# Down product of an expert block run one block later, behind gate and up of the next

## The reference, cut to what matters

```
def expert_block(args):
    xb_i, e = args
    h = jax.nn.silu(xb_i @ w_gate[e]) * (xb_i @ w_up[e])
    return h @ w_down[e]
yb = lax.map(expert_block, (xb, blk_e))
return jnp.zeros_like(x2d).at[t_s].add(yb[dest] * w_s[:, None])
```

## Time and profile before

| | us |
|---|---|
| median of 3 runs | 1984.62 (1983.09 to 1987.86) |
| time of the profiled execution | 1987.03 |
| its span, first to last instruction | 1985.3 |
| sixteen first blocks, sum of their lengths | 304.50 |
| sixteen second blocks | 297.59 |
| eight third blocks | 145.36 |

### The profile page before, as it was taken

One profiled execution on the slowest core, in us unless ns is written; L12 is line 12 of the kernel. 1 busy time (PEld: TensorE's weight loads), 2 busy tenths in 40 slices (PEclk: granted clock), 3 DMA queues, 4 the chain that ended last, 5 costly groups with the idle time before them and its releaser, 6 DMA issues. The chain is left out here.

```text
span 1985.3 us, 29116 instructions
## 1 busy us (share of the span) xinstructions
PE 1885.8 (95%) x10232; PEld 1609.0 (81%) x10233; DVE 1059.1 (53%) x2070; ACT 751.6 (38%) x1408; POOL 412.3 (21%) x571
## 2 busy tenths in 40 slices
PE   7899999999999999999999954999999999999996
PEld 5899987788888788888888853888888888888885
DVE  5634343545444654455453335576677666565572
ACT  4332323333334233333333213444465444444451
POOL 2000000000201001000001013444444434434443
PEclk9899999999999999999999956999999999999998
DMA  7222233422245223333223425587678857655552
GB/s 225 87 86 86 86 130 106 154 77 93 87 148 195 81 88 104 127 128 106 85 87 105 170 86 191 190 288 255 221 247 287 296 203 260 218 194 204 193 179 92
DMA packets 166566, 309.97 MB, mean 156 GB/s; under 512 B 18448, under 2 KB 85008, under 8 KB 166490
## 3 DMA queue, kind: packets, MB, share of 16 engines
q1 hardware_dynamic: 133706, 223.61, 32.8%
q0 software_dynamic: 32784, 85.33, 12.4%
HBM read 256.13 MB, written 83.69 MB: 171 GB/s over the span
## 5 line engine op out<-in xcount | busy, mean ns | idle before, releaser
L64 PE MATMUL bank<-xT_hi,wh 128*128 128x512 f32 (+1 forms) x960 | 340.8, 355 | 7.4 <-ACT S L751 5.4
L65 PE MATMUL bank<-xT_lo,wh 128*128 128x512 f32 (+1 forms) x960 | 340.4, 355 | 0.0
L66 PE MATMUL bank<-xT_hi,wl 128*128 128x512 f32 (+1 forms) x960 | 339.3, 353 | 0.0
L799 DVE TENSOR_TENSOR wl<-raw,wh 128x512 fp32r<-128x512 f32 x352 | 219.3, 684 | 201.7 <-ACT wh L602 201.6
L1776 PE MATMUL bank<-gu_hi,ex_hi 128*128 128x256 f32 (+1 forms) x960 | 313.9, 327 | 5.7 <-DVE gu_lo L1651 5.7
L1778 PE MATMUL bank<-gu_hi,ex_lo 128*128 128x256 f32 (+1 forms) x960 | 306.3, 319 | 0.0
L1777 PE MATMUL bank<-gu_lo,ex_hi 128*128 128x256 f32 (+1 forms) x960 | 306.2, 319 | 0.0
L602 ACT ACTIVATE wh<-raw 128x512 fp32r<-128x512 f32 x352 | 192.1, 619 | 85.2 <-PE bank L1223 54.7
L64 PEld LDWEIGHTS bank<-xT_hi,wh 128*128 128x128 f32 x960 | 182.3, 190 | 36.2 <-issue 9.8
L1776 PEld LDWEIGHTS bank<-gu_hi,ex_hi 128*128 128x128 f32 x960 | 182.7, 190 | 29.9 <-DVE gu_lo L1651 12.1
L66 PEld LDWEIGHTS bank<-xT_hi,wl 128*128 128x128 f32 x960 | 182.5, 190 | 25.5
(11 more groups left out here) (239 smaller groups left out, 3275.5 us busy)
## 6 DMA issues: line engine op xcount, KB each, us to landing
raw<-in_w_in SPq DMA_DIRECT2D x56, 1024.0 KB, 5.1
raw_gate_up<-in_w_gate SPq DMA_DIRECT2D x16, 2048.0 KB, 8.2
raw_gate_up<-in_w_up SPq DMA_DIRECT2D x16, 2048.0 KB, 9.5
raw_d<-in_w_down SPq DMA_DIRECT2D x16, 2048.0 KB, 10.1
raw<-in_w_out SPq DMA_DIRECT2D x16, 1024.0 KB, 6.3
raw<-in_w_up_pool SPq DMA_DIRECT2D x16, 512.0 KB, 3.4
raw<-in_w_up_gmlp SPq DMA_DIRECT2D x16, 512.0 KB, 4.6
h<-in_x_prompt SPq DMA_DIRECT2D x16, 512.0 KB, 5.0
```

What stands on the lines that cost most here:

```text
L64: nc.tensor.matmul(out, lh, rh, start=(i == 0), stop=False)
L65: nc.tensor.matmul(out, lh, rl, start=False, stop=False)
L66: last = nc.tensor.matmul(out, ll, rh, start=False, stop=(i == n - 1))
L799: lo = lambda out, x, hi: tt(out, x, hi.bitcast(F32), ALU.subtract)
```

## The change

The diff has these parts:

- PE: `down(j - 1)` stands behind gate, up and the row transposes of block j. All four hidden transposes of block j come after it, into one bank. Block 0 is written out ahead of the loop and has no down product; after the loop one more `down(total - 1)` follows.
- Up is one pass of 24 products of 512 columns into one bank, and hid is made by one DVE instruction once up is done.
- ACT and DVE make the parts of the transposed hidden rows of block j - 1 (`hidden_high`, `hidden_low`) in block j, in one instruction each. In a first block these stand behind the splits of gate and up.
- The down weights of a new expert are split at the end of its first block: ACT waits until the last down product of the expert before is done (`y_done`), since it now comes in that block.
- DVE: `scale(j + 1)` and then `rows_low(2 * j + 3)` stand behind hid in every block, first ones too, and the down split behind both.
- POOL: one more index tile and copy in each step (idx_2), and one more round at the end, since the rows lag by one block more.

```diff
@@ phase_three, POOL
+                    nc.gpsimd.tensor_copy(idx_2[:, :], idx_1[:, :]).then_inc(moved_2, 1)
+                    wait_apart(pool, moved_2, j, passed_pool)
                     nc.gpsimd.tensor_copy(idx_1[:, :], idx[:, :]).then_inc(moved, 1)
...
-                out_landed(total + 1)
-                wait_apart(pool, z_ok, 2 * total + 2, passed_pool)
...
+                for last, n in ((False, total + 1), (True, total + 2)):
+                    out_landed(n)
+                    wait_apart(pool, z_ok, 2 * n, passed_pool)
+                    nc.gpsimd.tensor_copy(idx_y[:, :], idx_h[:, :]).then_inc(moved_y, 1)
+                    root(n)
+                    wait_apart(pool, moved_y, n, passed_pool)
+                    if not last:
+                        next_h(n + 1, idx_1)
+                    store_final(n)
@@ phase_three, ACT
+                def hidden_high(j):
+                    act.wait_ge(th_done, j + 2)
+                    nc.scalar.activation(hT[0][:, :, :], bankH[:, :].rearrange("p (k i) -> p k i", k=KH),
+                                         ACT.Copy).then_inc(hT_hi, 1)
+
                 def per_block(e, i, lo, j, first=False):
+                    hidden_high(j - 1)
                     if not first:
                         use_sigmoid_table(0)
                         square(j + 1)
                     act.wait_ge(g_done, j + 1)
                     nc.scalar.activation(sg[:, :], bankG[:, :], ACT.Sigmoid).then_inc(sg_ok, 1)
+                    rows_high(j + 2)
                     if first:
+                        act.wait_ge(down_in, 16 * i + 16)
+                        act.wait_ge(y_done, lo + 2)
+                        for k in range(KH):
+                            nc.scalar.activation(dn[0][:, k, :], raw_d[:, k, :], ACT.Copy).then_inc(e_hi, 1)
@@ phase_three, DVE
                     if not first:
                         add(j + 1)
-                        mean(j + 1)
+                    hidden_low(j - 1)
+                    mean(j + 1)
                     dve.wait_ge(sg_ok, j + 1)
                     tt(sg[:, :], bankG[:, :], sg[:, :], ALU.mult)
                     dve.drain()
-                    dve.wait_ge(u1_done, j + 1)
...
+                    dve.wait_ge(gu_done, j + 2)
+                    tt(hid[:, :], bankU[:, :], sg[:, :], ALU.mult).then_inc(hid_ok, 1)
+                    scale(j + 1)
+                    rows_low(2 * j + 3)
                     if first:
...
+                        for k in range(KH):
+                            dve.wait_ge(e_hi, SPLITS_ACT * i + 2 * KD + k)
+                            lo_half(dn[1][:, k, :], raw_d[:, k, :], dn[0][:, k, :]).then_inc(e_lo, 1)
@@ phase_three, PE
+                def down(j):
+                    pe.wait_ge(z_ok, 2 * j + 4)
+                    pe.wait_ge(hT_lo, j + 2)
+                    for k in range(KH):
+                        for half in range(2):
+                            last = accumulate(bankY[half][:, :], hT, k, dn, k, slice(half * HALF, (half + 1) * HALF),
+                                              k, KH)
+                    last.then_inc(y_done, 1)
...
                     for k in range(KD):
                         pe.wait_ge(e_lo, SPLITS * i + KD + k + 1)
+                        last = accumulate(bankU[:, :], xT, k, gu, KD + k, slice(0, HALF), k, KD)
                     last.then_inc(gu_done, 1)
                     rows_of_x(16 * j + 32)
...
+                    if not begin:
+                        down(j - 1)
+                    hidden_transposed(j)
+                per_block(0, 0, 0, 0, first=True, begin=True)
+                experts(pe, lambda e, lo: None, per_block, peel=True, skip_first=True)
+                total = pe.value_load(blk_tab[0:1, 2 * NE - 1:2 * NE], min_val=1, max_val=MAXBLK)
+                down(total - 1)
```

More of the change, by code:

```diff
@@ L1627, in per_block @@
                     nc.scalar.activation(sg[:, :], bankG[:, :], ACT.Sigmoid).then_inc(sg_ok, 1)
[L1628 to L1639, removed]
+                    rows_high(j + 2)
                     if first:
-                        rows_high(j + 2)
+                        act.wait_ge(down_in, 16 * i + 16)
+                        act.wait_ge(y_done, lo + 2)
+                        for k in range(KH):
+                            nc.scalar.activation(dn[0][:, k, :], raw_d[:, k, :], ACT.Copy).then_inc(e_hi, 1)
                 experts(act, split, per_block, peel=True)
                 total = act.value_load(blk_tab[0:1, 2 * NE - 1:2 * NE], min_val=1, max_val=MAXBLK)
+                hidden_high(total - 1)
                 square(total + 1)
+                square(total + 2)
             @block.vector
@@ L1734, in per_block @@
                     dve.drain()
-                    dve.wait_ge(u1_done, j + 1)
[L1736 to L1739, removed]
-                    if first:
[L1741 to L1754, removed]
+                    dve.wait_ge(gu_done, j + 2)
+                    tt(hid[:, :], bankU[:, :], sg[:, :], ALU.mult).then_inc(hid_ok, 1)
+                    scale(j + 1)
+                    rows_low(2 * j + 3)
+                    if first:
+                        for k in range(KH):
+                            dve.wait_ge(e_hi, SPLITS_ACT * i + 2 * KD + k)
+                            lo_half(dn[1][:, k, :], raw_d[:, k, :], dn[0][:, k, :]).then_inc(e_lo, 1)
                 experts(dve, split, per_block, peel=True)
                 total = dve.value_load(blk_tab[0:1, 2 * NE - 1:2 * NE], min_val=1, max_val=MAXBLK)
-                add(total + 1)
-                mean(total + 1)
-                scale(total + 1)
+                hidden_low(total - 1)
+                for n in (total + 1, total + 2):
+                    add(n)
+                    mean(n)
+                    scale(n)
             @block.tensor
@@ L1778, in accumulate, with hidden_transposed, per_block @@
                     return nc.tensor.matmul(out, a[1][:, ka, :], w[0][:, kw, cols], start=False, stop=(n == total - 1))
[L1780 to L1783, removed]
+                def hidden_transposed(j):
+                    pe.wait_ge(hid_ok, j + 1)
+                    for k in range(KH):
+                        last = nc.tensor.transpose(bankH[:, k * P:(k + 1) * P], hid[:, k * P:(k + 1) * P], ident[:, :])
                     last.then_inc(th_done, 1)
[L1786 to L1791, removed]
+                def down(j):
+                    pe.wait_ge(z_ok, 2 * j + 4)
+                    pe.wait_ge(hT_lo, j + 2)
+                    for k in range(KH):
+                        for half in range(2):
+                            last = accumulate(bankY[half][:, :], hT, k, dn, k, slice(half * HALF, (half + 1) * HALF),
+                                              k, KH)
+                    last.then_inc(y_done, 1)
+                def per_block(e, i, lo, j, first=False, begin=False):
                     pe.wait_ge(ex_lo, 2 * j + 2)
-                    pe.wait_ge(hT_lo, 2 * j + 1)
                     for k in range(KD):
```

79 lines of the change are left out of this document (23 added, 56 removed).

## The result

| | before | after |
|---|---|---|
| median, same chip | 1986.24 us (1983.09 to 1988.08) | 2069.35 us (2068.25 to 2072.53) |
| span of the profiled execution | 1985.3 us | 2068.2 us |
| mean granted clock of PE over the span | 0.970 | 0.949 |

A forecast was written before the change was run, and what follows sets the result against it. PE, busy for 95% of the span, was taken to set the pace. First blocks +36, second 0, third -4, clock +6 and ends +10 summed to +48 us: 2033 us on the median, range 2004 to 2072.

The forecast's parts named there:

- The order on DVE in a first block: ex_lo behind scale, which waits for POOL's copy to idx_y: first blocks 21.3 us for 19.03, +36 us; bounds 17.7 and 22.9.
- the copy is then at 17.9: POOL's copy to idx_y in a first block comes 17.9 us after its first gate product, next gate product at 20.8.
- Second blocks: Down split at the end of first blocks delays the residual sum and scatter: 18.6 us, no change; bounds 17.7 and 20.
- The clock: PE idles before second blocks, so its clock may drop: a quarter of 1.5 us for sixteen waits, +6 us; bounds 0 and 24.
- rival 4: PE's clock falls at each wait and costs 1.5 us each time: +18 over the forecast, 2051 us; chance 0.12.
- Third blocks: Nothing late in an expert's third block: eight at 17.7 us, 141.6 in all, -4 us.
- the ends: The last down product and a second round of root, gather and stores lie open: +10 us; bounds +7 and +14.
- no wait for hT_lo: Down one block later ends PE's waits for hT_lo, removing up to 6.0 us that second blocks lose to waits.
- POOL's extra copy: Extra copy and wait in POOL's step, at most 1.1 us, hidden by its wait for the residual sum: nothing.
- Rival 3: Everything late, slow scatter landing in every block: first blocks 22.9, second 20 us; +96 us, 2081 us; chance 0.08.
- rival 1: Scatter takes its share beside the load, landing in 5.6 us: -8 us, 1977 us; chance 0.06.
- rival 2: Wait hidden altogether, scatter landing under 4.4 us, all 40 blocks at 17.7: 1959 us; chance 0.02.

The follow-up runs named there:

- experiment 1: Changed kernel with rows_low (ex_lo) ahead of scale in first blocks, scale last behind the down split: 2045.69 us, ratio to before 1.0301.
- experiment 2: Kernel before with scale put ahead of rows_low in first blocks, nothing else: 2053.53 us in one run.
- experiment 11: Kernel before with the copy to idx_y ahead of the wait for the scatter's landing and the next up load held until the down split is done: 2025.79 us.
- experiment 3: Changed kernel with 20 thrown-away products of 512 columns on PE behind a first block's hidden transposes: 2066.33 us in one run.
- experiment 6: Changed kernel with rows_low ahead of scale in first blocks, and up in two passes of 256 columns into two banks: 2060.15 us in one run.
- experiment 8: Changed kernel with the load of the next up weights held back until the down split is done: 2000.4 us in one run.
- experiment 10: Changed kernel with the copy to idx_y ahead of the wait for the scatter's landing and the next up load held until the down split: 1962.31 us, ratio 0.9866.
- each repair alone: Changed kernel with only the idx_y copy ahead of the wait for the scatter's landing, 2044.0 us; or only the up load held until the down split, 2000.4 us.

## Why the prediction was right or wrong

In all +82.9 us came for +48 forecast. The direction and the path are as predicted and the size is not: the time lies 3 us under the top of the range, whose spread went to 22.5 us for first blocks but only to 19.5 for second ones. That the range still holds it is in part luck.

**The order on DVE in a first block** decided it, as predicted. Experiments 1 and 2 show it from both sides, and the changed trace has each link. gu_lo starts 1.5 us ahead of block 26 (1.7 expected), the scatter goes out at 10.5 (10.3), and from the copy to the next gate product it is 2.8 us (2.9).

**The size of the first blocks is the mis-sized term.** +36 was forecast and +55.8 measured: 22.5 us each and not 21.3. The forecast counted sixteen late blocks; block 37 has no load and isn't late, so the other fifteen are at 22.84. The step that failed is "the copy is then at 17.9": it came at 20.0, because the landing took 9.5 us to the copy and not the 7.6 of the earlier trace rows. The load beside the scatter is the same one, as I argued, but the scatter is not. In the kernel before, a first block's scatter writes the rows of the block before, and behind a three-block expert that is a partly filled one (29 of 128 rows in block 26). With down one block later it writes a full block. The DMA lines of the two windows, before and then after (queue: packets, MB, share; below, the issue and its us to landing):

```profile
q0 software_dynamic: 288, 0.64, 15.0%
...
h_rows<-z_rows,idx_z POOLq DMA_INDIRECT x1, 7.4
```

```profile
q0 software_dynamic: 288, 1.05, 18.6%
...
h_rows<-z_rows,idx_z POOLq DMA_INDIRECT x1, 9.3
```

Over the first blocks of before, scatters with 2 to 32 valid rows land in 7.0 to 7.7 us and full ones in 8.6 to 9.6; in the changed kernel all have full blocks but that of block 0, and land in 8.8 to 9.7 (block 37, without a load, is left out in both). The place behind a three-block expert doesn't explain it, since full scatters have the same place in the changed kernel. So my upper bound, the 9.6 of the earlier trace rows, was the right row. This rests on counting rows, and no experiment changed their number alone. In first blocks of experiment 11, where the load of up is held back, scatters with 2 to 32 valid rows land in 2.2 to 2.6 us and full ones in 3.3 to 3.4, a step of 0.8 and not of 2.

**Second blocks** were forecast at 18.6 and measured at 20.0. In the block behind 26 the chain ran a little better than forecast: the sum starts at 4.4 us (4.7), the scatter at 7.0 (7.1), the copy comes at 13.8 (14.7), and no idle time follows. In the eight experts of two blocks it ran later: the scatter at 7.7 to 8.8, the copy at 15.0 to 16.6. What made the blocks of the first kind long is the clock, 2.1 us in the gate products of each; in the others the chain would have held them nearly as long (experiment 3).

**The clock** was forecast at +6, a quarter of 1.5 us a wait. By the trace it is 2.1 us for each of fifteen waits, some +32, as in rival 4 and beyond. Experiment 3 took most of it away, and the fifteen pairs became 11.5 us shorter: second blocks stand at 19.0, 0.4 above the forecast, and first ones at 23.1. So the term is some 6 us too small, and the trace alone would have led to a price nearly three times too high.

**Third blocks** (17.72 measured, 17.7 forecast; of this 0.33 for up in one pass, experiment 6, 0.3 forecast), **the ends** (+10.2, forecast +10), and **no wait for hT_lo** hold as written. **POOL's extra copy** was put at nothing because POOL waits for the residual sum anyway. In the second blocks of experts with a third one it still does, for 0.46 us. In the eight of two-block experts it no longer waits there, so the cover is gone, and up to the 1.1 us a step that the prediction names can lie in the chain; no run takes the copy out.

**Rivals.** Rival 3, everything late, is the nearest, 12 us too high: some 6 in first blocks (22.9 for 22.5, nearly all of it block 37), and another 6 for the clock, which is inside the 20 of its second blocks already. Rivals 1 and 2 needed a landing under 6.1 and 4.4 us. Only block 37 and experiments 8 and 10 have it, with the load out of the way. The Trainium skill (DMA: Bandwidth & Descriptors, Queues, rings and completion order) has a DMA engine take turns between queues with work; the estimate that I drew from it, at most 5.6 us, doesn't hold here: 8.8 to 9.7 beside one load against 3.3 alone.

**Open.** Whether the number of valid rows by itself makes the step from 7.4 to 9.3 us, and why block 0's scatter, with no valid row, still takes 7.3 beside a load.

## What to carry to other kernels

When an instruction is moved or reordered on an in-order engine, look at what then stands behind each wait, and price the wait by its worst row, not by the one at hand: the moved step may carry other data. A stall with two dependents only pays when both are freed or its cause is removed: here each repair alone left the kernel slower than before (by 2.9%, and by 0.7% in one run), and the two together made it 1.3% faster. Before a slowdown behind a wait is charged to the clock, fill the wait and see whether the time comes back, block by block, since filler also costs where there was no wait.

## What the runs showed of the hardware

- A scatter of 128 z_rows by POOL's queue lands in 3.3 us alone and in 8.8 to 9.7 issued 0.9 us behind a 2 MB load; the load's own landing in block 26 differs too, 8.9 us in the kernel before and 11.9 in the changed one.
- Each of PE's waits of 4.3 to 6.1 us comes with a stretch of 3.4 or 6.8 us at a granted clock of 0.50 that reaches into the products behind it, and the 24 gate products there take 2.1 us longer. With the waits filled the fifteen pairs of blocks were 11.5 us shorter and not 32.
- A copy of 128x3 numbers on POOL takes 0.18 us, and 2.28 us beside DVE's split of the gate and up weights (idx_z, in all sixteen first blocks of either kernel).
